# Making the low halves of two of four weight tiles with a negated copy on ScalarE and an adding DMA of GpSimd, in a two-block transformer kernel

## The chip, the cores and the metric

The kernel runs on one core of a Trainium2 chip. The metric is the device time of one execution in microseconds, the median of several runs. Beside it stands one profiled execution, whose span runs from the first to the last instruction.

## The reference

Two transformer blocks follow one another on one sequence of 512 tokens with 2048 channels, all in float32. What matters here is the first block and in it the "fox" attention: eight heads of width 128, each with four projections of the normalised input (query, key, value, output gate), causal scores with a bias from cumulated forget gates, a softmax, and the gated product.

```
h = rmsnorm(x, norm_g[l])
proj = h @ w_in[l]
cv_a, cv_b, cv_gate, fq, fk, fv, f_logit, fox_gate, mq, mem_gate = jnp.split(proj, SPLITS, axis=-1)
...
s = jnp.einsum('bqhd,bkhd->bhqk', qi, k) * scale
p = jax.nn.softmax(where(mask, s + bias, -inf), axis=-1)
y_fox = einsum('bhqk,bkhd->bqhd', p, v) * jax.nn.silu(fox_gate)
```

Beside it the first block has a causal convolution over 31 taps and an attention over a memory, and the second block a banded attention and a linear recurrence. Each column of every projection costs the same kind of work: a 2048 by 128 weight tile against all 512 tokens.

## The kernel before

**A product in three matmuls.** Float32 products are made from two rounded halves. A weight tile `raw` (128 partitions by 2048 floats, 1 MB) is split into `w_hi`, its rounding to the matmul's float32r, and `w_lo = raw - w_hi`. The input stands in SBUF as `act_hi` and `act_lo`. `project` on TensorE takes 16 steps over the channels with three matmuls each: `act_hi` by `w_hi`, `act_lo` by `w_hi`, `act_hi` by `w_lo`. It waits once, ahead of its first weight load, for the semaphore `w_split`, which counts whole split tiles. So a tile's low half must be there before its first matmul.

**How a tile comes in.** There are two slots of `raw`, `w_hi` and `w_lo`, used in turn. For tile t: SyncE loads `raw` (`load`, three tiles ahead, so it waits until tile t-2 is split, since that one stands in the same slot); ScalarE copies `raw` to `w_hi` (`split` in the scalar block) once TensorE has finished tile t-2; VectorE subtracts (`split` in the vector block) and counts `w_split` up; TensorE starts tile t when tile t-1 is through. Between the end of tile t-2 and the start of tile t lies one projection's time, or more where other matmuls are put between.

**A head of the fox phase.** It has four tiles, called 0 to 3 here; tile 4 is tile 0 of the next head. Each engine has its own program, a loop over the eight heads. `split(i, j)` makes tile j+1. Scores and transposes are put between the steps of tiles 2 and 3 (hooks), and `weigh`, the probabilities by the values, stands behind tile 3. VectorE has, beside the splits, the scaling of query and key, the softmax, four `ada_step` calls of two pieces (a product of a streamed weight of the second block with a vector, L2029), and convolution taps (L1868). SyncE's queue is in written order: `load` of tile 3 and its two `ada` pieces, `load` of tile 4 and two pieces, and so on. GpSimd has nothing in this phase.

Of the kernel before, what the change touches and what calls it, by code (L numbers as in the profile page):

```python
# [82 lines left out]
TILE0 = {}  # L83
# [69 lines left out]
def build(nc, wt, ada, bias, xT, memT, pw, cols_d, consts_d, starts_d, masks_d, spill, c_row, cum_rows, out):  # L153
    ctx = ExitStack()
    with ctx:
        def sb(name, shape, dt=F32, stack=ctx):
            return stack.enter_context(nc.sbuf_tensor(name, shape, dt))

        def sem(name):
            return ctx.enter_context(nc.semaphore(name))  # L160
# [10 lines left out]
        raw = sb("raw", [P, 2, D])  # L171
        w_hi = sb("w_hi", [P, 2, D], F32R)
        w_lo = sb("w_lo", [P, 2, D], F32R)
        cols = sb("cols", [P, NCOLS])
        consts = sb("consts", [P, CONSTS])
        masks = sb("masks", [P, 2 + NLEV, P], BF16)
# [123 lines left out]
        first_hi = sem("first_hi")  # L300
        first_split = sem("first_split")
        quad_done = sem("quad_done")
        s_x = [sem(f"s_x{n}") for n in range(4)]
        s_raw = [sem("s_raw0"), sem("s_raw1")]
        s_ada = [sem("s_ada0"), sem("s_ada1")]
        s_stage = [sem("s_stage0"), sem("s_stage1")]
# [134 lines left out]
                pair_turned)]  # L441
        own = {n: sem(f"own_{n}") for n in ("act", "dve", "pool")}

        s_block = [sem(f"s_block{n}") for n in range(4)]
        block_sum = Count(sem("block_sum"), fast=4)
        block_hi = Count(sem("block_hi"), fast=7)
        block_split = Count(sem("block_split"), fast=7)
# [52 lines left out]
        def tile_no(phase, i, j):  # L500
            return PHASES[phase][1] * i + (TILE0[phase] + j)
# [5 lines left out]
        def slot(phase, j):  # L507
            return (TILE0[phase] + j) % 2
# [689 lines left out]
        def _(act):  # L1198
# [4 lines left out]
            def split(phase, i, j, ahead=1):  # L1203
# [6 lines left out]
                act.wait_ge(proj_done, t if not isinstance(t, int) else max(t, 1))  # L1210
                fn(w_hi[:, s, :], raw[:, s, :], ACT.Copy).then_inc(w_hi_done, 1)  # L1211

            def rows(dst, src, width, tmp):

                o.step(fn(tmp, src, ACT.Ln, scale=1.0 / width, bias=eps_c))
                o.settle()
                return fn(dst, tmp, ACT.Exp, scale=-0.5)
# [183 lines left out]
            def fox(i):  # L1401
                split("fox", i, 0)
                split("fox", i, 1)
                high("fox", i, 0, qk_hi, qkv)
                split("fox", i, 2)
                high("fox", i, 1, qk_hi, qkv)
                for t in range(QT):
                    exps("fox", i, t, tp[:, 0, :])
                value_out("fox", i, 2, qkv[:, 2, :])
                split("fox", i, 3)  # L1410
                act.wait_ge(side_full.sem, side_full.at("fox", i, 1))
                o.step(fn(qkv[:, 3, S - P:S], ps_x[:, S - P:S], ACT.Copy))
                fn(v_hi[:, 0:S - P], ps_x[:, 0:S - P], ACT.Copy).then_inc(value_high.sem, 1)
                for j in range(QT):
                    probsT_fox(i, j)
                gate_exp("fox", i, 3, dst=2, src=wk[:, 1, :])
# [271 lines left out]
            def block_high(p, n):  # L1688

                if n in (1, 4, 6):  # L1690
                    f, k = ((0, 0), None, None, (0, 1), None, (1, 1))[n - 1]
                    if p:
                        act.wait_ge(s_block[2 * f + k], 16 * p)
                    else:
                        act.wait_ge(s_raw[slot("fast", f)], 16 * (half("fast", 0, f) + 1))
                else:
                    act.wait_ge(block_sum.sem, block_sum.at("fast", p, (2, None, 1, 3, None, 4)[n]))
                fast_slot_free(act, p, n)
                fn(fast_slot(n, w_hi), FAST_FROM[n], ACT.Copy).then_inc(block_hi.sem, 1)  # L1699
# [18 lines left out]
        def _(dve):  # L1718
# [325 lines left out]
                return TAPS_FOX * i + (TAPS0 + TAPS_MEM * NMEMH + n)  # L2044

            def fox(i):
                split("fox", i, 0)
                ada_step("fox", i, 0)
                conv_tap(fox_tap(i, 0))
                dve.wait_ge(proj_done, tile_no("fox", i, 0) + 2)  # L2050
                do(stt(qkv[:, 0, :], ps_p[:, slot("fox", 0), :], SCALE, r1[:, :], ALU.mult, ALU.mult))
                dve.sem_inc(evac[slot("fox", 0)], 1)
                dve.sem_inc(qk_in.sem, 1)
                split("fox", i, 1)
                ada_step("fox", i, 1)
                conv_tap(fox_tap(i, 1))
                low("fox", i, 0, qk_lo, qkv, qk_hi)
                o.settle()
                dve.wait_ge(proj_done, tile_no("fox", i, 1) + 2)
                do(tt(qkv[:, 1, :], ps_p[:, slot("fox", 1), :], r1[:, :], ALU.mult))  # L2060
                dve.sem_inc(evac[slot("fox", 1)], 1)
                dve.sem_inc(qk_in.sem, 1)
                dve.tensor_copy(tp[:, 1, 0:P], qkv[:, 1, 0:P]).then_inc(first_ready.sem, 1)
                split("fox", i, 2)
                dve.wait_ge(first_ready.sem, first_ready.at("fox", i, 1))
                low("fox", i, 1, qk_lo, qkv, qk_hi)
                o.settle()
                dve.sem_inc(qk_ready.sem, 1)
                for t in range(QT):
                    soft_in("fox", i, t, lambda t, e: stt(e, ps_s[:, t % 2, 0:P * (t + 1)], cn[:, t, bass.ds(i, 1)],  # L2070
                                                          Y[:, 4 + i, 0:P * (t + 1)], ALU.add, ALU.subtract))
                for t in range(QT):
                    soft_out("fox", i, t)
                ada_step("fox", i, 2)
                split("fox", i, 3)
                conv_tap(fox_tap(i, 2))
                value_lo("fox", i, v_lo, v_hi)
                for j in range(QT - 1):
                    dve.wait_ge(probsT_ready.sem, probsT_ready.at("fox", i, j + 1))
                    tt(p_lo[j], p_raw[j], turned(tp_r)[j].bitcast(F32), ALU.subtract).then_inc(probs_low.sem, 1)  # L2080
                silu_z("fox", i, 3, wk[:, 2, :], between=lambda: ada_step("fox", i, 3))
                ada_out("fox", i)
                dve.wait_ge(heads_full.sem, heads_full.at("fox", i, 1))
                tt(Y[:, 4 + i, :], ps_o[:, :], wk[:, 3, :], ALU.mult).then_inc(heads_done.sem, 1)
# [27 lines left out]

            dve.wait_ge(heads_done.sem, heads_done.at("fox", 7, 1))
            channels_added(Y)
            split("gate", 0, 0)
            dve.wait_ge(side_full.sem, side_full.at("gate", 0, 1))
            do(ts(ssq_b[:, :], ps_x[:, :], 1.0 / (NCONV * P), None, ALU.mult))
# [408 lines left out]
            def first_sums(p, n):  # L2526
                if n == 0:
                    if p:
                        dve.wait_ge(s_block[2], 16 * p)
                        dve.wait_ge(s_block[3], 16 * p)  # L2530
                        dve.wait_ge(block_split.sem, block_split.at("fast", p - 1, 5))
                    else:
                        for f in range(2):
                            dve.wait_ge(s_raw[slot("fast", f)], 16 * (half("fast", 0, f) + 1))
                    tt(block_sums[0], raw_block(1, 0), raw_block(1, 1), ALU.add).then_inc(block_sum.sem, 1)
                else:
                    if p:
                        dve.wait_ge(s_block[0], 16 * p)
                        dve.wait_ge(block_split.sem, block_split.at("fast", p - 1, 7))
                    dve.wait_ge(block_sum.sem, block_sum.at("fast", p, 1))  # L2540
                    tt(block_sums[1], block_sums[0], raw_block(0, 0), ALU.add).then_inc(block_sum.sem, 1)  # L2541

            def last_sums(p, n):
                if n == 2:
                    dve.wait_ge(block_split.sem, block_split.at("fast", p, 3))
                    tt(block_sums[0], raw_block(0, 0), raw_block(1, 0), ALU.add).then_inc(block_sum.sem, 1)
                else:
                    if p:
                        dve.wait_ge(s_block[1], 16 * p)
                    dve.wait_ge(block_split.sem, block_split.at("fast", p, 1))  # L2550
                    tt(block_sums[1], block_sums[1], raw_block(0, 1), ALU.add).then_inc(block_sum.sem, 1)

# [83 lines left out]
        def _(pool):  # L2636
# [19 lines left out]
            for k in range(KT):  # L2656
                if k % 4 == 0:
                    pool.wait_ge(s_mem[k // 4], 16)
                m = mem_raw[:, k, :]
                if k == 0:  # L2660
                    o.step(tt(mem_total, m, m, ALU.mult))
                    o.settle()
                    pool.sem_inc(mem_sq, 1)
                    pool.sem_inc(mem_added, 1)
                else:
                    o.step(tt(mem_norm, m, m, ALU.mult))
                    o.settle()
                    pool.sem_inc(mem_sq, 1)
                    o.step(tt(mem_total, mem_total, mem_norm, ALU.add))
                    o.settle()  # L2670
                    pool.sem_inc(mem_added, 1)

            def out1(i):

# [155 lines left out]
```

## Time and profile before

| | |
|---|---|
| median of 3 runs | 1859.9 us (1859.87 to 1860.23) |
| span of the profiled execution | 1857.9 us; 2.0 us lie around it |
| TensorE busy | 1851.6 us, 100% of the span |
| VectorE, ScalarE, GpSimd busy | 1285.2, 830.6, 210.6 us (69%, 45%, 11%) |
| fox phase | eight heads of 48.9 us, from about 251.9 to 643.4 us |
| HBM read | 235.75 MB |

Busy shares alone say which engine could be the bound, not which wait ends last at a given tile. That is read in the stretch of one head, from rows in order of time: a line there gives start, length, engine, source line, what is written from what, and in brackets the idle time before it and what ended it.

### The profile page before, as it was taken

What the parts mean: (1) busy time and instruction counts of PE and PEld (TensorE: products, weight loads), DVE (VectorE), ACT (ScalarE), POOL (GpSimd) and SP (SyncE); (2) the same over time, 40 slices, a digit from 0 to 9 for tenths busy, and PEclk for the clock granted to TensorE, in tenths of its full rate; (3) what the DMA queues carried; (4) which work ended last, traced back from release to release, by engine and by line L of the source; (5) the groups of instructions that cost most, each with busy time, mean ns of one, the idle gap of its engine ahead of it and who ended that gap; (6) DMA issues with size and microseconds to landing.
All of it is one profiled execution on the core that took longest, in us unless ns stands there. A gap on an engine that the chain in (4) does not pass through costs nothing.

```text
span 1857.9 us, 26478 instructions
## 1 busy us (share of the span) xinstructions
PE 1851.6 (100%) x9142; PEld 1553.5 (84%) x9142; DVE 1285.2 (69%) x1847; ACT 830.6 (45%) x1227; POOL 210.6 (11%) x203
## 2 busy tenths in 40 slices
PE   9999999999999999999999999999999999999999
PEld 8888888888888887887788888888888888888999
DVE  6766678888888877667844444455566666659986
ACT  6543433333333373233644444444555455557333
POOL 3500000000000003443000000000222222111111
PEclk9999999999999999999999999999999999999999
DMA  7344145444444435765222222221212212223442
GB/s 285 113 151 189 68 159 181 172 160 165 178 160 160 179 114 196 247 239 201 87 83 93 93 92 72 93 93 68 85 74 90 90 68 90 79 80 127 150 155 92
DMA packets 52002, 244.85 MB, mean 132 GB/s; under 512 B 5864, under 2 KB 7400, under 8 KB 32624
## 3 DMA queue, kind: packets, MB, share of 16 engines
q1 hardware_dynamic: 51504, 241.02, 36.7%
q10 hardware_dynamic: 448, 3.17, 0.4%
q8 instruction: 31, 0.51, 0.1%
q14 instruction: 19, 0.16, 0.0%
HBM read 235.75 MB, written 8.41 MB: 131 GB/s over the span
## 4 chain that ended last, share of the span: by engine, by line
PE 94%; DVE 4%; issue 1%; ACT 1%; POOLq 0%; DVEq 0%; another core or an unknown queue 0%; ACTq 0%
PE ps_p L729 25%; PE ps_p L731 25%; PE ps_p L730 25%; PE ps_o L894 1%; PE ps_s L1090 1%; PE ps_t L1188 1%; PE ps_t L1189 1%; PE ps_t L1187 1%; PE ps_t L878 1%; PE ps_s L1188 1%; PE ps_s L1187 1%; PE ps_s L1189 1%; PE ps_x L748 1%; DVE act_lo L2238 1%; PE ps_s L868 0%
## 5 line engine op out<-in xcount | busy, mean ns | idle before, releaser
L729 PE MATMUL ps_p<-act_hi,w_hi 128*128 128x512 f32 x2080 | 832.6, 400 | 0.3 <-DVE w_lo L1739 0.3
L731 PE MATMUL ps_p<-act_hi,w_lo 128*128 128x512 f32 x2080 | 812.0, 390 | 0.0
L730 PE MATMUL ps_p<-act_lo,w_hi 128*128 128x512 f32 x2080 | 810.6, 390 | 0.0
L731 PEld LDWEIGHTS ps_p<-act_hi,w_lo 128*128 128x128 f32 x2080 | 390.4, 188 | 85.2
L729 PEld LDWEIGHTS ps_p<-act_hi,w_hi 128*128 128x128 f32 x2080 | 391.0, 188 | 75.2 <-issue 1.2
L730 PEld LDWEIGHTS ps_p<-act_lo,w_hi 128*128 128x128 f32 x2080 | 391.4, 188 | 73.4 <-issue 0.7
L1211 ACT ACTIVATE w_hi<-raw 128x2048 fp32r<-128x2048 f32 x141 | 269.5, 1912 | 270.1 <-PE ps_p L731 251.4
L1734 DVE TENSOR_TENSOR w_lo<-raw,w_hi 128x2048 fp32r<-128x2048 f32 x139 | 318.7, 2293 | 72.2 <-ACT w_hi L1211 60.5
L2029 DVE CUSTOM_DVE_ANT_0 mkv<-mkv,c_all 128x1024 f32<-128x1024 f32 x96 | 146.0, 1557 | 3.3 <-DVE wk L1776 2.9
L2677 POOL TENSOR_TENSOR ssq_a<-ssq_a,wk 128x512 f32<-128x512 f32 x15 | 36.3, 2420 | 724.8 <-ACT wk L1475 724.8
L2697 POOL TENSOR_TENSOR hz<-hqk,hd 128x128 f32<-128x128 f32 x48 | 34.2, 713 | 728.6 <-DVEq L2403 690.0
L2251 DVE TENSOR_TENSOR sq_lo<-wk,sq_hi 128x512 fp32r<-128x512 f32 x24 | 16.6, 692 | 109.1 <-ACT sq_hi L1541 83.4
L1371 ACT ACTIVATE tp<-tp,stat 128x128 f32<-128x128 f32 (+1 forms) x64 | 35.9, 561 | 114.9 <-DVE stat L1998 114.9
L1868 DVE SCALAR_TENSOR_TENSOR Y<-upad,cols,Y 128x512 f32<-128x512 f32 x120 | 82.0, 745 | 0.0
L1744 DVE SCALAR_TENSOR_TENSOR wk<-ps_p,wk 128x512 f32<-128x512 f32 x23 | 15.9, 691 | 54.1 <-ACT wk L1228 54.1
L1699 ACT ACTIVATE w_hi<-mkv 128x1024 fp32r<-128x1024 f32 x24 | 25.5, 1061 | 62.1 <-DVE mkv L2541 32.9
L1539 ACT ACTIVATE wk<-ps_p 128x512 f32<-128x512 f32 x15 | 9.0, 597 | 85.1 <-PE ps_p L731 84.0
L1239 ACT ACTIVATE wk<-wk 128x512 f32<-128x512 f32 x43 | 27.2, 632 | 37.9 <-DVE wk L1783 20.5
L1626 ACT ACTIVATE hz<-hd 128x256 f32<-128x256 f32 x48 | 20.2, 422 | 49.5 <-DVE hd L2393 30.2
L1228 ACT ACTIVATE wk<-wk,cols 128x512 f32<-128x512 f32 (+1 forms) x53 | 38.4, 724 | 1.7
L1222 ACT ACTIVATE wk<-ps_p 128x512 f32<-128x512 f32 x32 | 19.0, 594 | 38.3 <-PE ps_p L731 38.3
L1226 ACT ACTIVATE wk<-wk 128x512 f32<-128x512 f32 (+1 forms) x53 | 33.5, 632 | 1.7
(435 smaller groups left out, 2578.5 us busy)
## 6 DMA issues: line engine op xcount, KB each, us to landing
raw<-wt_dram SPq DMA_DIRECT2D x146, 1024.0 KB, 4.8
mkv<-ada_dram SPq DMA_DIRECT2D x96, 512.0 KB, 4.4
raw<-wt_dram SPq DMA_DIRECT2D x20, 512.0 KB, 4.8
qkv<-xT_dram SPq DMA_DIRECT2D x16, 256.0 KB, 2.9
spill_dram<-Y SPq DMA_DIRECT2D x16, 256.0 KB, 2.2
out_dram<-wk SPq DMA_DIRECT2D x15, 256.0 KB, 2.1
Y<-xT_dram SPq DMA_DIRECT2D x3, 1024.0 KB, 10.7
mem_raw<-memT_dram SPq DMA_DIRECT2D x4, 512.0 KB, 11.9
```

The lines of the kernel that those rows point to most:

```text
L729: mm(o, wh, hi[:, k, 0:n], start=at == 0, stop=False)
L730: mm(o, wh, lo[:, k, 0:n], start=False, stop=False)
L731: last = mm(o, wl, hi[:, k, 0:n], start=False, stop=at == KT - 1)
L1187: mm(o, wh[:, c], hi[:, k, :], start=n < 3 and k == 0, stop=False, skip_group_check=True)
L1188: mm(o, wh[:, c], lo[:, k, :], start=False, stop=False, skip_group_check=True)
L1189: last = mm(o, wl[:, c], hi[:, k, :], start=False, stop=k == HALF_K - 1, skip_group_check=True)
L1211: fn(w_hi[:, s, :], raw[:, s, :], ACT.Copy).then_inc(w_hi_done, 1)
L1228: return fn(dst, dst, ACT.Ln, bias=one_c[0:dst.shape[0], :])
L1734: tt(w_lo[:, s, :], raw[:, s, :], w_hi[:, s, :].bitcast(F32), ALU.subtract).then_inc(w_split, 1)
L1868: o.step(stt(Y[:, c, :], upad[:, c, bass.ds(tap, S)], cols[:, bass.ds(tap + (w0 + c * TAPS), 1)], Y[:, c, :], ALU.mult, ALU.add))
L2029: dve.tensor_tensor_reduce(out=w, in0=w, in1=c_all[:, n % 2 * ADA_PIECE:(n % 2 + 1) * ADA_PIECE], scale=1.0, scalar=0.0, op0=ALU.mult, op1 ...
L2677: o.step(tt(ssq_a[:, :], ssq_a[:, :], wk[:, j, :], ALU.add))
```

## The change

For tiles 2 and 4 of each fox head VectorE no longer subtracts. ScalarE writes the negated rounding, `-w_hi`, into `w_lo` right behind its copy to `w_hi` (`negate`), and GpSimd issues a DMA from SBUF to SBUF that adds `raw` to `w_lo` (`accum_op=ALU.add`), waits for it to land, waits that the tile before has been counted, and counts `w_split` up. VectorE waits for that count before the splits that follow, so that the count stays in order. Tiles 1 and 3, and all other phases, are as before. To make room for two semaphores, the last phase takes over four that the memory's loads used (its waits are 16 higher), and an unused one is dropped.

```diff
+        ADDED = (1, 3)
-        s_block = [sem(f"s_block{n}") for n in range(4)]
+        s_block = s_mem
+        negated = Count(sem("negated"), fox=2)
+        s_low_added = sem("s_low_added")
...
+            def negate(phase, i, j):
+                s = (TILE0[phase] + j + 1) % 2
+                fn(w_lo[:, s, :], raw[:, s, :], ACT.Copy, scale=-1.0).then_inc(negated.sem, 1)
...
             def fox(i):
                 split("fox", i, 0)
                 split("fox", i, 1)
+                negate("fox", i, 1)
                 high("fox", i, 0, qk_hi, qkv)
...
                 split("fox", i, 3)
+                negate("fox", i, 3)
                 act.wait_ge(side_full.sem, side_full.at("fox", i, 1))
...
             def fox(i):
+                dve.wait_ge(w_split, tile_no("fox", i, 0) + 2)
                 split("fox", i, 0)
...
-                split("fox", i, 1)
                 ada_step("fox", i, 1)
...
+                dve.wait_ge(w_split, tile_no("fox", i, 2) + 2)
                 split("fox", i, 2)
...
                 ada_step("fox", i, 2)
-                split("fox", i, 3)
                 conv_tap(fox_tap(i, 2))
...
+            dve.wait_ge(w_split, tile_no("gate", 0, 0) + 2)
             split("gate", 0, 0)
...
+            def fox(i):
+
+                for n, j in enumerate(ADDED):
+                    s = slot("fox", j + 1)
+                    pool.wait_ge(negated.sem, negated.at("fox", i, n))
+                    pool.dma_start(w_lo[:, s, :], raw[:, s, :], accum_op=ALU.add).then_inc(s_low_added, 16)
+                    pool.wait_ge(s_low_added, 32 * i + 16 * n + 16)
+                    pool.wait_ge(w_split, tile_no("fox", i, j + 1) + 1)
+                    pool.sem_inc(w_split, 1)
+            for i in range(PHASES["fox"][0]):
+                fox(i)
```

**ScalarE, the first half of a fox head.** The rows below are the program of before, in order; `w_hi<-raw` is a split's copy, `qk_hi<-qkv` the rounding of the query, and `tp,stat` the first exponential.

```order
L1210 REGISTER_ALU [waits s_raw1]
L1211 ACTIVATE w_hi<-raw 128x2048 [waits proj_done]
L1397 REGISTER_ALU
L1399 ACTIVATE qk_hi<-qkv 128x384 [waits qk_in]
L1209 ISA
```

And the same place in the changed program.

```order
L1213 REGISTER_ALU [waits s_raw1]
L1214 ACTIVATE w_hi<-raw 128x2048 [waits proj_done]
L1218 ACTIVATE w_lo<-raw 128x2048
L1404 REGISTER_ALU
L1406 ACTIVATE qk_hi<-qkv 128x384 [waits qk_in]
```

A copy of the same shape, with no wait of its own, now stands between the split of tile 2 and the rounding of the query.

**ScalarE, the second half of a head.** The changed program around the split of tile 4; `v_hi` is the rounded value tile, `tp_r` the rounded transposed probabilities.

```order
L1214 ACTIVATE w_hi<-raw 128x2048 [waits own_act,proj_done,s_raw1]
L1218 ACTIVATE w_lo<-raw 128x2048
L1420 REGISTER_ALU
L1421 ACTIVATE qkv<-ps_x 128x128 [waits side_full]
L1422 ACTIVATE v_hi<-ps_x 128x384
```

The row of L1218 is new there too, ahead of `v_hi`.

**VectorE, around the key of a head.** Before, the split of tile 3 stands right behind the key's copy.

```order
L2060 TENSOR_TENSOR qkv<-ps_p,r 128x512 [waits proj_done,own_dve]
L2063 COPY tp<-qkv 128x128 [waits own_dve]
L1733 REGISTER_ALU
L1734 TENSOR_TENSOR w_lo<-raw,w_hi 128x2048 [waits w_hi_done]
```

Now it has a wait for tile 2's count ahead of it.

```order
L2069 TENSOR_TENSOR qkv<-ps_p,r 128x512 [waits proj_done,own_dve]
L2072 COPY tp<-qkv 128x128 [waits own_dve]
L2073 REGISTER_ALU
L1742 REGISTER_ALU [waits w_split]
L1743 TENSOR_TENSOR w_lo<-raw,w_hi 128x2048 [waits w_hi_done]
```

Two of a head's four rows of that shape on VectorE are gone (those of tiles 2 and 4), and both that stay wait for `w_split`.

## Rows read from the trace of the kernel before

**Rows 1.** Page: busy time and share; granted TensorE clock in 40 slices

```profile
PE 1851.6 (100%) x9142; PEld 1553.5 (84%) x9142; DVE 1285.2 (69%) x1847; ACT 830.6 (45%) x1227; POOL 210.6 (11%) x203
PEclk9999999999999999999999999999999999999999
```

**Rows 2.** Windows of a head each: engines' busy us, clock, DMA share, GB/s

```profile
545.50:594.50 49.00, 49.00 (x232) 40.75 (x230) 41.71 (x72) 18.43 (x29) 0.00 (x0) 1.00 0.49 171
...
sum 391.50, PE 391.50 PEld 325.44 DVE 330.99 ACT 146.76 POOL 0.00; mean PE 48.94 PEld 40.68 DVE 41.37 ACT 18.34 POOL 0.00
```

**Rows 3.** TensorE's waits, whole run: total us, times, longest (first and last)

```profile
PE ps_o L754 <- DVE wk L1720: 1.1, 1, 1.1
...
PE ps_o L1006 <- ACT wk L1501: 0.2, 1, 0.2
```

**Rows 4.** TensorE's weight loads that begin tile 2 and the next tile 0

```profile
567.18 0.19 PEld L729 LDWEIGHTS ps_p<-act_hi,w_hi 128*128 128x128 f32 x1
...
594.42 0.19 PEld L729 LDWEIGHTS ps_p<-act_hi,w_hi 128*128 128x128 f32 x1
```

**Rows 5.** ScalarE in order of time, one head

```profile
556.72 1.92 ACT L1211 ACTIVATE w_hi<-raw 128x2048 fp32r<-128x2048 f32 x1 [6.13 <-PE ps_p L731]
558.90 0.53 ACT L1399 ACTIVATE qk_hi<-qkv 128x384 fp32r<-128x384 f32 x1 [0.26 <-DVEq L2053]
...
582.65 1.92 ACT L1211 ACTIVATE w_hi<-raw 128x2048 fp32r<-128x2048 f32 x1 [0.25 <-ACT qkv L1387]
584.47 0.26 ACT L1412 ACTIVATE qkv<-ps_x 128x128 f32<-128x128 f32 x1
584.62 0.48 ACT L1413 ACTIVATE v_hi<-ps_x 128x384 fp32r<-128x384 f32 x1
586.74 0.69 ACT L1377 ACTIVATE tp_r<-ps_t,r1c 128x512 fp32r<-128x512 f32 x1 [1.63 <-PE ps_t L878]
...
588.36 0.59 ACT L1378 ACTIVATE tp<-ps_t,r1c 128x384 f32<-128x384 f32 x1
```

**Rows 6.** TensorE's transposes of probabilities, same head

```profile
589.89 0.27 PE L878 MATMUL ps_t<-consts,tp 128*128 128x128 f32 x1
```

**Rows 7.** VectorE in order of time, one head

```profile
559.03 2.29 DVE L1734 TENSOR_TENSOR w_lo<-raw,w_hi 128x2048 fp32r<-128x2048 f32 x1 [0.33 <-DVE qkv L2051]
...
566.19 0.55 DVE L1986 TENSOR_TENSOR qk_lo<-qkv,qk_hi 128x384 fp32r<-128x384 f32 x1
...
569.55 2.29 DVE L1734 TENSOR_TENSOR w_lo<-raw,w_hi 128x2048 fp32r<-128x2048 f32 x1 [0.71 <-ACT w_hi L1211]
```

**Rows 8.** VectorE's subtractions in the fox phase: duration ns min/median/max

```profile
L1734 DVE TENSOR_TENSOR w_lo<-raw,w_hi x32: 2281/2292/2294, 256.7 to 634.2; 128x2048 fp32r<-128x2048 f32 x32
```

**Rows 9.** Page: DMA issues, KB each, median us from issue to landing

```profile
raw<-wt_dram SPq DMA_DIRECT2D x146, 1024.0 KB, 4.8
mkv<-ada_dram SPq DMA_DIRECT2D x96, 512.0 KB, 4.4
```

**Rows 10.** SyncE's queue in order of time, one head

```profile
561.50 0.33 SPq L574 DMA_DIRECT2D raw<-wt_dram  x1
...
572.01 0.33 SPq L574 DMA_DIRECT2D raw<-wt_dram  x1
584.39 1.48 SPq L601 DMA_DIRECT2D mkv<-ada_dram  x2
587.74 0.33 SPq L574 DMA_DIRECT2D raw<-wt_dram  x1
```

**Rows 11.** Windows: one 1 MB load alone, then the stretch from 586.4

```profile
572.00:573.00 1.00, 1.00 (x8) 0.85 (x6) 0.45 (x1) 0.00 (x0) 0.00 (x0) 1.00 0.22 33
573.00:574.00 1.00, 1.00 (x9) 0.87 (x8) 0.56 (x2) 0.00 (x0) 0.00 (x0) 1.00 0.51 115
574.00:576.00 2.00, 2.00 (x12) 1.74 (x11) 1.77 (x7) 0.50 (x2) 0.00 (x0) 1.00 1.01 426
...
586.40:587.60 1.20, 1.20 (x10) 1.02 (x9) 1.20 (x2) 0.86 (x2) 0.00 (x0) 1.00 1.26 321
```

More of the change, by code:

```diff
@@ L302, in build @@
         quad_done = sem("quad_done")
-        s_x = [sem(f"s_x{n}") for n in range(4)]
+        s_x = [None, sem("s_x1"), sem("s_x2"), sem("s_x3")]
         s_raw = [sem("s_raw0"), sem("s_raw1")]
@@ L1692, in block_high @@
                     if p:
-                        act.wait_ge(s_block[2 * f + k], 16 * p)
+                        act.wait_ge(s_block[2 * f + k], 16 * p + 16)
                     else:
@@ L2528, in first_sums @@
                     if p:
-                        dve.wait_ge(s_block[2], 16 * p)
-                        dve.wait_ge(s_block[3], 16 * p)
+                        dve.wait_ge(s_block[2], 16 * p + 16)
+                        dve.wait_ge(s_block[3], 16 * p + 16)
                         dve.wait_ge(block_split.sem, block_split.at("fast", p - 1, 5))
@@ L2537, in first_sums @@
                     if p:
-                        dve.wait_ge(s_block[0], 16 * p)
+                        dve.wait_ge(s_block[0], 16 * p + 16)
                         dve.wait_ge(block_split.sem, block_split.at("fast", p - 1, 7))
@@ L2548, in last_sums @@
                     if p:
-                        dve.wait_ge(s_block[1], 16 * p)
+                        dve.wait_ge(s_block[1], 16 * p + 16)
                     dve.wait_ge(block_split.sem, block_split.at("fast", p, 1))
```

## The prediction, made before the changed kernel ran

> **What bounds the kernel now.** I read the busy shares first: TensorE is busy 1851.6 of 1857.9 us, and its granted clock stands in the top tenth in all 40 slices [rows 1]. VectorE, the engine that the change relieves, is at 69%. Busy shares are means over stages, so I then read the fox phase by itself. In each of the eight head windows TensorE is busy all the time, 391.50 of 391.50 us, VectorE 330.99, ScalarE 146.76, and GpSimd not at all [rows 2]. Last I read TensorE's waits. The whole run has six of them, from 1.1 us down to 0.2 [rows 3], and the same view over the fox phase alone has no line. So no low half comes late today. VectorE's subtraction for tile 2 runs from 559.03 to 561.32, and TensorE asks for that tile at 567.18, where it loads the first weights [rows 4, 7]. The slack is 5.9 us.
>
> From that follows the first half of the forecast: there is nothing to win at these sixteen tiles. A faster VectorE would end nothing sooner, because nobody waits for it. What the change can do is lose time, if the new way to the low half takes longer than its slack.
>
> **What is taken away.** Two subtractions a head of 2.292 us [rows 8], sixteen in all, 36.7 us of VectorE's time, none of it on the path. VectorE's work falls from 41.4 to about 36.8 us of a head's 48.9. I cost it at 0 both ways: the taps and pieces that follow only run earlier, and their ends are not waited for.
>
> **What ScalarE gets.** One more activation of the same shape as the copy, 1.92 us with the next one starting 1.82 us after it [rows 5], sixteen times. Cover: for tile 2 it runs from 558.54 to 560.46, so the rounding of the query moves from 558.90 to about 560.4. Its reader is the subtraction at 566.19 [rows 7], 5 us of room. For tile 4 it runs from 584.47 to 586.39. The value's two copies move from 584.47 to 586.3 and end near 586.95, where the first probabilities are taken at 586.74 now: 0.2 us later. Two copies further the end at 588.95 becomes 589.15, and the transpose that waits for it starts at 589.89 [rows 5, 6]. So 0.7 us of room is left; I cost it at 0. If it were gone, each tenth of a microsecond of lateness would be 0.8 us over eight heads.
>
> **What the DMA has to meet.** Tile 2: the negated copy ends at 560.46 and TensorE asks at 567.18, so 6.7 us remain for GpSimd to wake, issue, move 1 MB with an addition, see it land and count. Tile 4: 586.39 to 594.42, 8.0 us [rows 4, 5]. This is the term on which all rests, and no trace row shows it: there is no DMA of GpSimd, none from SBUF to SBUF and none that adds. I bound it by the nearest row, SyncE's load of the same 1 MB: 4.8 us from issue to landing [rows 9]. The load at 572.01 [rows 10] shows what these 4.8 us are made of. For about 1 us hardly anything moves, for another 1 us the DMA engines are half busy at 115 GB/s, and then they stream at 426 GB/s, at which 1 MB is 2.46 us [rows 11].
>
> Lower bound: it costs what a load costs, 4.8 us, landing at 565.3, 1.9 us ahead of need. Upper bound by rows: an addition has to read both its operands, so the stream is twice as long, 4.8 + 2.46 = 7.3 us; with some 0.1 us for GpSimd's counting, tile 2 comes 0.7 us late. At tile 4 two `ada` pieces are issued just ahead, by 585.9, and the engines are full with them until 587.6 and beyond [rows 10, 11]. I put 1 us on it: 586.39 + 8.3 + 0.1 = 594.8, 0.4 us late. That is 1.1 us a head, 8.8 us in all.
>
> Between them I take the doubled stream without most of the slow second microsecond, since the source is not HBM, about 0.6 us less, but with GpSimd's issue 0.2 us dearer than SyncE's: 6.9 us. Tile 2 is ready at 567.4 to 567.5, 0.2 to 0.3 us late; tile 4 at 594.4, on time. Eight heads at 0.25 us are 2 us at most, and half of that if the first weight load hides behind the matmuls still in flight. I take +1.2 us.
>
> The Trainium skill bears on this twice. Its page "Collectives: The Full Stack" (Part 3, on the bandwidth ceiling) says that the reduce step runs at half the rate of the copy step because the adding descriptor has two source reads on the same ring, not because the addition costs anything. No run here shows it yet; by it the stream is the doubled one. Its page "DMA: Bandwidth & Descriptors" (Anatomy of one DMA) gives for GpSimd's DMAs 2.0 us plus bytes by 436 GB/s, which with two reads of 1 MB is an estimate of 6.8 us, and it (SWDGE vs HWDGE) speaks against the change in that only GpSimd's software path can accumulate at all, with a first byte at about 1 us against 0.6.
>
> **What waits behind the new waits.** VectorE's split of tile 3 now waits for tile 2's count. It starts at 569.55 today [rows 7], so a DMA that lands by 569.5 does not hold it; behind it stand the key's low half and the softmax, which the scores between tile 2's steps need. On SyncE, the load of tile 4 goes from 561.50 to about 567.4 and that of the tile after next from 587.74 to about 594.4 [rows 10], and the `ada` pieces behind them with it. The first is read at 582.65, 15 us later; the second by the next head's split at 605.66, one head of 48.94 us behind the row at 556.72 [rows 2, 5], 11 us later. With 4.8 us to land both are hidden. The later load also leaves the DMA engines to the adding transfer. The `ada` pieces behind the second come up to one load's stream, 2.46 us, later than now; VectorE, which reads them, has 4.6 us a head to spare. I cost it at 0.
>
> **The sum.** Span 1857.9 + 0 (VectorE) + 0 (ScalarE) + 1.2 (DMA) = 1859.1 us, and with the 2.0 us that lie between span and median, 1861.1 us. What a measurement of this kernel can tell from no change is about 0.2%, 3.7 us.
>
> **Rivals.**
> *Late by the whole doubled stream or somewhat more.* If neither the start-up nor anything else is saved, 8.8 us come on top as worked out, 1868.7 us; with 1 us more for GpSimd's issue, 2 us more per head, 1885. For it: the doubled stream is plain, and the slack of tile 2 is only 6.7 us. It decides slower from 0.47 us of lateness per head on, a DMA of about 7.1 us. This is the rival on the other side. Chance 0.34.
> *The adding DMA is another kind of slow* (its engines do not stream at 426 GB/s at all). If its stream took four times a copy's, 9.8 us, the DMA is 12.2 us: tile 2 late by 5.6, tile 4 by 5.3, some 11 us a head, 87 us in all, 1947. Nothing in the trace speaks for it, nothing excludes it. At three times, 1908. Chance 0.12.
> *VectorE's relief shows somewhere.* It would need TensorE to be held by VectorE in the fox phase or at its end. TensorE has no wait in this phase, and the longest of the run is 1.1 us [rows 3]. If that one went, it would be 1859.9 - 1.1 = 1858.8 us. Chance of more than 0.2%: 0.03.
> *ScalarE's added copy holds the scores or transposes.* The room is 0.7 us, and at 1 us of extra lateness it would cost 2.4 us; it lies within the first two cases.
>
> **How the numbers follow.** Just in time or all but, within 0.2%: 0.51, and its own range is 1859.4 to 1863.6. Late by up to 2 to 3 us a head: 0.34, 1863.6 to 1885. Much later: 0.12. Faster by over 0.2%: 0.03. The range of 8 in 10 runs from 1859.3 to 1885: below it is hardly anything, above it the third case and the tail of the second. Faster 0.03, same 0.51, slower 0.46.
>
> **What would show it.** In the fox windows of the changed kernel VectorE's busy time falls to about 36.8 us a head and ScalarE's rises to about 22.3. GpSimd's DMAs appear, 16 of 1 MB, with about 6.9 us to landing: 4.8 would say one read is enough, 7.3 the upper bound, over 9 the third case. TensorE's waits have a line for the first matmul of a tile, released by GpSimd, of some tenths of a microsecond and at most 16 times, or none. If waits of over 0.5 us stand there, the rival holds; if the wait falls on a score or a transpose instead, the ScalarE step is wrong. A granted clock below the top tenth in these slices would be something that I have left out.

## The result and the profile after

The changed kernel takes 1872.3 us (median of 4 runs, 1871.33 to 1872.81) against 1860.07 us (1859.87 to 1860.68): the ratio is 1.0066, 95% interval 1.0051 to 1.008, some 12.2 us slower. The profiled execution has a span of 1869.5 us, 11.6 us more than before, at a granted clock of 1.0.

The page of the changed kernel, to be read against [rows 1, 9]: busy time, the queue of GpSimd's DMAs (packets, MB, share of 16 engines), and issues with median us to landing.

```profile
PE 1856.3 (99%) x9142; PEld 1554.1 (83%) x9142; DVE 1251.7 (67%) x1831; ACT 857.5 (46%) x1243; POOL 224.7 (12%) x219
...
q0 software_dynamic: 2304, 16.78, 4.4%
...
raw<-wt_dram SPq DMA_DIRECT2D x146, 1024.0 KB, 4.8
mkv<-ada_dram SPq DMA_DIRECT2D x96, 512.0 KB, 5.4
w_lo<-raw POOLq DMA_DIRECT2D x16, 1024.0 KB, 7.6
```

VectorE is busy 33.5 us less, where 36.7 us of subtractions were taken away; no run looked into the other 3 us. TensorE became busier by 4.7 us with the same 9142 matmuls, and its span grew by 11.6. A matmul that starts behind a pause shows a longer time, so busy time alone does not show where the rest went. TensorE's waits over the fox phase, an empty answer before, do:

```profile
PE ps_p L732 <- POOLq L2691: 7.3, 16, 0.9
```

L732 is the first matmul of a projection step and L2691 GpSimd's count of `w_split`. The row gives total, number of waits and the longest, and all sixteen tiles are waited for. One head in order of time, tile 2 first, from ScalarE's and GpSimd's rows and TensorE's matmuls and weight loads:

```profile
567.48 1.90 ACT L1218 ACTIVATE w_lo<-raw 128x2048 fp32r<-128x2048 f32 x1
...
569.67 0.86 POOL L2688 DMA_DIRECT2D w_lo<-raw  x1 [22.96 <-ACT w_lo L1218]
...
576.11 0.39 PE L734 MATMUL ps_p<-act_hi,w_lo 128*128 128x512 f32 x1
576.68 0.50 PE L732 MATMUL ps_p<-act_hi,w_hi 128*128 128x512 f32 x1 [0.19 <-POOLq L2691]
...
576.68 0.19 PEld L732 LDWEIGHTS ps_p<-act_hi,w_hi 128*128 128x128 f32 x1 [0.61 <-POOLq L2691]
```

The negated copy ends at 569.38 and GpSimd's DMA starts at 569.67: 0.29 us go for the wake-up. The next matmul follows after 0.57 us instead of the usual 0.23, so 0.34 us are lost ahead of it, and another 0.11 us behind it, where the matmul after it starts 0.34 us later instead of 0.23. The bracket on the matmul says only 0.19, because the one before it is still drawn as running. The weight load's bracket says 0.61. Before, that load started together with the last matmul of the tile ahead [rows 4]; now it starts with its own matmul. So a wait row gives less than the loss: 7.3 us in the list. The starts of the matmuls themselves give 4.05 us at tile 2's eight places and 7.53 at tile 4's, together the 11.6 us of the span.

Then tile 4 of the same head:

```profile
596.08 0.86 POOL L2688 DMA_DIRECT2D w_lo<-raw  x1 [25.55 <-ACT w_lo L1218]
...
603.72 0.38 PE L900 MATMUL ps_o<-tp,qkv 128*128 128x128 f32 x2
604.44 0.49 PE L732 MATMUL ps_p<-act_hi,w_hi 128*128 128x512 f32 x1 [0.34 <-POOLq L2691]
```

0.72 us between these two starts, where it was 0.14; this is the mildest of the eight. How long the DMAs take tells the two tiles apart: 6.9 to 7.0 us at tile 2, 8.2 to 8.8 at tile 4. The line of GpSimd's issue gives shortest, median and longest of all sixteen, and the windows show the DMA engines, first for tile 2's DMA and then for tile 4's. A window's line gives its stretch and length, the busy time of TensorE's matmuls and weight loads, VectorE, ScalarE and GpSimd, the clock, the DMA engines' share and the GB/s.

```profile
DMA to landing us min/median/max: 6.9/7.6/8.8
...
569.70:571.10 1.40, 1.40 (x7) 1.15 (x7) 1.40 (x3) 0.08 (x1) 0.83 (x1) 1.00 0.03 6
571.10:576.30 5.20, 5.20 (x24) 4.13 (x22) 2.74 (x5) 0.00 (x0) 0.00 (x0) 1.00 0.99 200
...
596.10:598.00 1.90, 1.90 (x12) 1.54 (x11) 1.80 (x4) 1.90 (x5) 0.84 (x1) 1.00 0.93 257
598.00:604.00 6.00, 6.00 (x32) 4.98 (x30) 2.88 (x5) 2.44 (x6) 0.00 (x0) 1.00 0.91 203
```

At tile 2 next to nothing moves for 1.4 us after the issue. Then the engines are full for 5.2 us, and the view credits them with 200 GB/s, where a load ran at 426 [rows 11]. 1 MB at 200 GB/s is 5.2 us, twice a load's 2.46. At tile 4 the engines are at work already when the DMA is issued.

### The profile page after: what moved, and what is told of

Read it like the earlier page. It is cut to its first block, busy times and chain, and to the rows that moved or that the text cites. A ratio compares the mean times of both kernels' runs of the same rounds, so it can differ in the third digit from the quotient of the medians.

```text
span 1869.5 us, 26503 instructions
## 1 busy us (share of the span) xinstructions
PE 1856.3 (99%) x9142; PEld 1554.1 (83%) x9142; DVE 1251.7 (67%) x1831; ACT 857.5 (46%) x1243; POOL 224.7 (12%) x219
## 3 DMA queue, kind: packets, MB, share of 16 engines
q0 software_dynamic: 2304, 16.78, 4.4%
## 4 chain that ended last, share of the span: by engine, by line
PE 60%; DVE 4%; ACT 1%; issue 1%; DVEq 0%; another core or an unknown queue 0%; ACTq 0%
PE ps_p L732 16%; PE ps_p L734 16%; PE ps_p L733 16%; PE ps_s L1093 1%; PE ps_t L1191 1%; PE ps_t L1192 1%; PE ps_t L1190 1%; PE ps_s L1191 1%; PE ps_s L1190 1%; PE ps_s L1192 1%; PE ps_o L897 1%; DVE act_lo L2248 1%; PE ps_t L881 0%; DVE w_lo L2565 0%; ACT act_hi L1654 0%
## 5 line engine op out<-in xcount | busy, mean ns | idle before, releaser
L732 PE MATMUL ps_p<-act_hi,w_hi 128*128 128x512 f32 x2080 | 833.6, 401 | 7.7 <-POOLq L2691 7.3
L732 PEld LDWEIGHTS ps_p<-act_hi,w_hi 128*128 128x128 f32 x2080 | 391.0, 188 | 87.2 <-issue 7.1
L1743 DVE TENSOR_TENSOR w_lo<-raw,w_hi 128x2048 fp32r<-128x2048 f32 x123 | 282.1, 2293 | 70.0 <-ACT w_hi L1214 59.9
L2038 DVE CUSTOM_DVE_ANT_0 mkv<-mkv,c_all 128x1024 f32<-128x1024 f32 x96 | 146.6, 1557 | 15.2 <-DMA mkv<-ada_dram 11.8
L2688 POOL DMA_DIRECT2D w_lo<-raw x16 | 13.9, 868 | 554.4 <-ACT w_lo L1218 554.4
```

The source lines that it names most:

```text
L732: mm(o, wh, hi[:, k, 0:n], start=at == 0, stop=False)
L1743: tt(w_lo[:, s, :], raw[:, s, :], w_hi[:, s, :].bitcast(F32), ALU.subtract).then_inc(w_split, 1)
L2038: dve.tensor_tensor_reduce(out=w, in0=w, in1=c_all[:, n % 2 * ADA_PIECE:(n % 2 + 1) * ADA_PIECE], scale=1.0, scalar=0.0, op0=ALU.mult, op1 ...
```

## The experiments

Theory A: the loss is the adding DMA's lateness at TensorE, tile by tile. Theory B: ScalarE's added copies do it. The third question was whether VectorE's freed time is worth anything. Every kernel was timed beside the kernel before on the same chip; its median there was 1860.03 to 1860.10 us.

### One tile at a time

```diff
-        ADDED = (1, 3)
+        ADDED = (1,)
...
-                negate("fox", i, 3)
...
                 ada_step("fox", i, 2)
+                split("fox", i, 3)
```

> Only tile 2 of each head gets its low half by the adding DMA; VectorE subtracts tile 4 again. Theory A, the loss is the lateness of the DMA, tile by tile: in the changed kernel's trace the eight gaps ahead of tile 2 are 0.34 to 0.52 us longer than a normal step, and the matmul after each comes 0.11 us later, together about 4.0 us, so 1860.1 + 4.0 = 1864.1 us. GpSimd's DMA takes 6.9 us as before. Theory B, ScalarE's added copies hold the scores or transposes and the waits only look like the DMA's: half of the loss, 1866, and the gaps ahead of tile 2 change. If the two tiles' losses were not additive, this and the run with tile 4 alone would not sum to 12.2 us.

Measured: 1864.37 us, ratio 1.0023 (1.0014 to 1.0032), 4.3 us lost. The eight DMAs take 6.9 to 7.0 us, and the waits row is

```profile
PE ps_p L732 <- POOLq L2691: 1.9, 8, 0.4
```

The reverse, `ADDED = (3,)` with VectorE's `split("fox", i, 1)` put back:

> Only tile 4 of each head gets its low half by the adding DMA; VectorE subtracts tile 2 again. Theory A: the gaps ahead of tile 4 in the changed kernel were 0.6 to 1.2 us against 0.14 normally, in sum 6.5 us and some 0.9 more behind them, so about 1867.6 us; the DMA takes 8.2 to 8.8 us there, because two ada pieces are in the DMA engines with it. Theory B: 1866.

Measured: 1866.31 us, ratio 1.0032 (1.002 to 1.0044), 6.3 us lost, DMAs of 7.9 to 8.8 us. The first is near theory A's 1864.1 and not theory B's 1866. The second lies 1.3 us under theory A's 1867.6 and next to theory B's 1866, so by its size it does not tell the two apart. That is done by two runs further below, the plain copy and ScalarE's copies alone. The two losses sum to 10.6 us, not 12.2. The 1.6 us between are less than the intervals of these runs, some 2 us each way, and in the profiled executions nothing is left over: their spans are 4.5 and 7.7 us longer than before, and 11.6 with both.

### A copy instead of an addition

```diff
-                    pool.dma_start(w_lo[:, s, :], raw[:, s, :], accum_op=ALU.add).then_inc(s_low_added, 16)
+                    pool.dma_start(w_lo[:, s, :], raw[:, s, :]).then_inc(s_low_added, 16)
```

> The DMA of GpSimd copies raw into w_lo and does not add, so the low halves of these sixteen tiles are wrong and the output is not the reference's; everything else stays. Theory A with the doubled read: the packets go from 0.64 us to about 0.31, the DMA from 6.9 to about 4.4 us at tile 2 and from 8.4 to about 6 at tile 4, no wait of TensorE is left, 1860.1 us. Rival, the cost is GpSimd's software issue or the conversion to float32r and not the second read: packets stay at 0.6 us and the time at 1872.

Measured: 1859.99 us, ratio 0.9999 (0.999 to 1.0008). The loss is gone. The DMA's share in the page, the issue's line, and the windows of one DMA at tile 2:

```profile
q0 software_dynamic: 2304, 16.78, 2.3%
...
L2688 POOL DMA_DIRECT2D w_lo<-raw x16: 530/530/722, 267.2 to 635.6; - x16
...
DMA to landing us min/median/max: 4.1/5.1/6.5
...
560.70:561.80 1.10, 1.10 (x7) 0.90 (x6) 1.09 (x3) 0.14 (x1) 0.53 (x1) 1.00 0.00 0
561.80:564.50 2.70, 2.70 (x14) 2.23 (x13) 2.70 (x6) 0.00 (x0) 0.00 (x0) 1.00 1.00 388
```

Same source, same target, same conversion to float32r, same issuer, same 2304 packets: the addition alone raises the stream from 2.7 to 5.2 us and the start from 1.1 to 1.4. The issue itself takes 530 ns against 859. So an adding DMA of 1 MB costs 2.8 us more than a copying one (6.9 against 4.1). The run does not tell whether it is the second read or the adding itself that doubles the stream.

### The negated copy first

```diff
                 act.wait_ge(proj_done, t if not isinstance(t, int) else max(t, 1))
+                if negated_first:
+                    negate(phase, i, j)
                 fn(w_hi[:, s, :], raw[:, s, :], ACT.Copy).then_inc(w_hi_done, 1)
...
-                split("fox", i, 1)
-                negate("fox", i, 1)
+                split("fox", i, 1, negated_first=True)
...
                     pool.wait_ge(w_split, tile_no("fox", i, j + 1) + 1)
+                    pool.wait_ge(w_hi_done, tile_no("fox", i, j + 1) + 2)
                     pool.sem_inc(w_split, 1)
```

(`split("fox", i, 3)` likewise.)

> Both tiles by the adding DMA as in the changed kernel, but ScalarE writes the negated copy first and w_hi behind it, so the DMA starts 1.8 us earlier and w_hi is ready 1.8 us later, still 4.8 us ahead of need. Theory A: tile 2 is then 1.3 us early and tile 4 about 0.9 us early, no wait is left, and the time is that of the kernel before, 1860.1 us; VectorE's 36.7 us less work win nothing. Rival, VectorE's relief is worth something that the waits hid: clearly under 1860. Theory B, ScalarE's extra copy costs by itself: it stays at 1866 or more, as ScalarE has the same work at the same places.

Measured: 1860.69 us, ratio 1.0004 (0.9995 to 1.0013). All sixteen adding DMAs are there, the list of TensorE's waits in the fox phase is empty, and the time is that of the kernel before within the interval. The page:

```profile
PE 1852.8 (100%) x9142; PEld 1554.1 (84%) x9142; DVE 1251.5 (67%) x1831; ACT 857.7 (46%) x1243; POOL 224.5 (12%) x219
...
w_lo<-raw POOLq DMA_DIRECT2D x16, 1024.0 KB, 8.8
```

The DMAs are even slower here than in the changed kernel, 8.8 us in the median against 7.6. They start while more of the other loads are under way: at tile 4 of the head shown above the two `ada` pieces are issued 0.5 us ahead of the DMA instead of 2.3. They cost next to nothing all the same, because they start 1.8 us earlier. The list leaves out short waits; by the matmuls' starts three of the eight tiles 4 still come late. The first and worst, 0.43 us between two starts instead of 0.14:

```profile
300.90 0.38 PE L900 MATMUL ps_o<-tp,qkv 128*128 128x128 f32 x2
301.33 0.49 PE L732 MATMUL ps_p<-act_hi,w_hi 128*128 128x512 f32 x1
```

The three add up to 0.6 us. So even the swapped order has no room left at tile 4. And VectorE is relieved by the same 34 us as in the changed kernel, with no gain.

### The `ada` pieces out of the way

```diff
-                    ada_piece(ADA_PER[phase] * i + (ADA_G0[phase] + n + 2), n % 2)
+                    ada_piece(ADA_PER[phase] * i + (ADA_G0[phase] + n + 2), n % 2, 128 if phase == "fox" and j == 2 else ADA_PIECE)
```

> The changed kernel, with the two ada pieces that SyncE loads just ahead of tile 4's adding DMA cut from 1024 to 128 columns each, so the second block's modulation is computed from stale numbers and the output is not the reference's. Theory A with contention: tile 4's DMA takes 6.9 to 7.1 us, as tile 2's does, instead of 8.2 to 8.8, lands ahead of need, and only tile 2's waits are left: 1864.1 us. Rival, tile 4's DMA is longer for another reason (ScalarE's and VectorE's work beside it): it stays at 8.4 us and 1872.

Measured: 1864.43 us, ratio 1.0023 (1.0013 to 1.0032), and the issue's line and the waits row are

```profile
DMA to landing us min/median/max: 6.9/6.9/7.0
...
PE ps_p L732 <- POOLq L2691: 1.8, 8, 0.4
```

All sixteen DMAs now take the 6.9 us of one alone, tile 4 is in time, and tile 2's loss stays, 4.3 us, as in the run with tile 2 alone. ScalarE's and VectorE's work beside tile 4's DMA is that of the changed kernel, so it is not what makes that DMA longer.

### In halves

```diff
-                fn(w_lo[:, s, :], raw[:, s, :], ACT.Copy, scale=-1.0).then_inc(negated.sem, 1)
+                for c in (slice(0, BLOCK), slice(BLOCK, D)):
+                    fn(w_lo[:, s, c], raw[:, s, c], ACT.Copy, scale=-1.0).then_inc(negated.sem, 1)
...
+                    for h, c in enumerate((slice(0, BLOCK), slice(BLOCK, D))):
+                        pool.wait_ge(negated.sem, negated.at("fox", i, 2 * n + h))
+                        pool.dma_start(w_lo[:, s, c], raw[:, s, c], accum_op=ALU.add).then_inc((s_low_added, s_low_second)[h], 16)
                     pool.wait_ge(s_low_added, 32 * i + 16 * n + 16)
+                    pool.wait_ge(s_low_second, 32 * i + 16 * n + 16)
```

> The negated copy in two halves of 1024 columns and an adding DMA of 512 KB behind each, so the first starts some 0.9 us earlier. If the stream of packets is what takes the time: both halves together land about 0.7 us earlier, tile 2 is in time and tile 4 late by 0.3, 1860.1 + 2.5 = 1862.6 us. Rival, each DMA of GpSimd pays its start of 1.4 us in turn and ScalarE pays for two shorter copies: no gain, 1872 or more.

Measured: 1871.57 us, ratio 1.006 (1.0046 to 1.0074). A miss: the total is near the rival's 1872, but its cause does not fit either, since tile 2 does gain. The waits row and two rows of GpSimd and TensorE:

```profile
PE ps_p L733 <- POOLq L2695: 10.8, 8, 1.6
...
595.89 1.81 POOL L2691 DMA_DIRECT2D w_lo<-raw  x2 [24.12 <-ACT w_lo L1220]
...
605.99 0.49 PE L733 MATMUL ps_p<-act_hi,w_hi 128*128 128x512 f32 x1 [1.21 <-POOLq L2695]
```

Only tile 4 is still waited for: at tile 2 the earlier start works. At tile 4 ScalarE's split began at 592.73 here and at 592.06 in the changed kernel. Counted from it the first DMA is issued after 3.16 us instead of 4.02, yet TensorE starts after 13.26 instead of 12.38. A start 0.9 us earlier ended 0.9 us later. The windows from the first issue on show where the time goes:

```profile
595.90:597.00 1.10, 1.10 (x8) 0.92 (x8) 1.10 (x3) 1.10 (x4) 1.01 (x2) 1.00 0.91 361
597.00:598.00 1.00, 1.00 (x8) 0.82 (x7) 1.00 (x2) 1.00 (x3) 0.70 (x1) 1.00 1.44 139
598.00:599.00 1.00, 1.00 (x6) 0.78 (x5) 0.75 (x3) 1.00 (x3) 0.00 (x0) 1.00 0.37 94
```

From 597 to 599 little moves, 139 and 94 GB/s. The adding DMA's first packet comes at 598.99, 3.1 us after its issue; at tile 2 of this kernel it comes after 1.4 us, and at tile 4 of the changed kernel after 1.5 to 2.2. So at tile 4 the halves lose their lead in a late start of the stream. What holds the stream back beside the `ada` pieces stays open.

### ScalarE's copies alone

```diff
                 split("fox", i, 1)
+                negate("fox", i, 1)
...
+                dve.wait_ge(negated.sem, negated.at("fox", i, 0))
                 split("fox", i, 1)
```

(the same at tile 4, on the kernel before)

> The kernel before, with ScalarE's sixteen negated copies into w_lo added at the places of the changed kernel; VectorE waits for each and then subtracts over it, there is no DMA of GpSimd. The two splits of VectorE come up to 1.5 us later. Theory A: nothing waits for either, 1860.1 us. Theory B, the added copies delay the query's rounding, the value and the transposes: up to 1866, with waits of TensorE on scores, transposes or values.

Measured: 1860.71 us, ratio 1.0004 (0.9994 to 1.0013). TensorE is busy through the whole phase, with ScalarE at 173.22 us against 146.76 [rows 2]:

```profile
251.90:643.40 391.50, 391.50 (x1826) 325.46 (x1825) 330.57 (x562) 173.22 (x242) 0.00 (x0) 1.00 0.47 169
```

So theory B is out: the copies by themselves cost nothing that this run can tell from noise.

### The tile with the most room

Tile 3 alone, `ADDED = (2,)`, with `negate("fox", i, 2)` behind the key's rounding and the three other subtractions on VectorE.

> Only tile 3 of each head gets its low half by the adding DMA; VectorE subtracts the others. Tile 3 has the longest room, since scores stand between the steps of tile 2: the negated copy ends about 573.3 in the time frame of the kernel before, the DMA takes 6.9 us, no ada piece is in its way, and TensorE asks at about 581.5. Theory A, only the room counts: it lands by 580.6, no wait, 1860.1 us. Rival, at this place ScalarE's copy does hold the key's rounding and with it the second scores: waits of TensorE on a score, and 1861.5 or more.

Measured: 1860.9 us, ratio 1.0005 (0.9996 to 1.0014), DMAs of 6.9 to 7.7 us, no wait in the fox phase. At this tile the DMA fits as it is.

### Tile 2 in time, tile 4 as it was

The negated copy goes first for tile 2 alone; tile 4 is as in the changed kernel.

> Both tiles by the adding DMA; ScalarE negates first for tile 2 alone, so that tile 2's DMA is there but in time, and tile 4 is as in the changed kernel. Tile 4 alone cost 6.3 us, both together 12.2, tile 2 alone 4.3, so 1.6 us are left over. If they come from tile 2 being late (it shifts what follows in the head), this run loses 6.3 us, 1866.3. If they come from tile 2's DMA being there at all (it holds SyncE's loads back, so that ada pieces come later), it loses about 7.9 us, 1868.0.

Measured: 1866.17 us, ratio 1.0033 (1.002 to 1.0045). 6.1 us lost, as with tile 4 alone. The median is next to the first expectation, 1866.3, but the interval, 3.7 to 8.4 us lost, holds the second too, so the run does not decide what the 1.6 us are, or whether they are more than scatter. Tile 4's DMA takes 8.5 us in the mean of eight in the changed kernel, 8.4 here and 8.3 with tile 4 alone, and from head to head it varies by more than that (8.2 to 8.8, 8.2 to 8.6 and 7.9 to 8.8 us).

## Why the prediction was right in part

**The bound and the missing gain were right.** TensorE was full in this phase and nobody waited for the sixteen subtractions. Two kernels that keep VectorE's relief and have no late DMA, or three by 0.1 to 0.3 us, take 1860.69 (negated first) and 1859.99 us (plain copy), like the kernel before. So the rival that VectorE's relief shows somewhere is refuted, and the 33.4 to 33.7 us that VectorE is busy less in them are worth nothing here.

**ScalarE's copy at 0 was right**, shown by its run alone.

**The DMA was sized right and judged late by too little.** I had taken 6.9 us between 4.8 and 7.3, and alone it takes 6.9 to 7.0. Its doubled stream is shown by the plain copy, and what the Trainium skill says in "Collectives: The Full Stack" on the two source reads fits with that trace, 5.2 us against 2.7; no run separates the second read from the adding. What failed is the step from there to "Tile 2 is ready at 567.4 to 567.5, 0.2 to 0.3 us late; tile 4 at 594.4, on time", and the 1.2 us put on it. Three terms were too small or missing:

- The wake-up of GpSimd, 0.29 us from the end of the copy to the issue. I had only 0.1 us, for the count at the end.
- Tile 2: with it the loss is 4.3 us over eight heads, 0.54 a head against 0.25 at most. With the wake-up put in, the prediction's own slack gives it: in the head shown the weight load comes 0.57 us later than it could (576.68 instead of 576.11). The assumption that half would hide behind the matmuls in flight was wrong, since 0.45 us of these 0.57 are lost: 0.34 ahead of the first matmul and 0.11 behind it.
- Tile 4: two `ada` pieces ahead of it cost 1.0 to 1.9 us (7.9 to 8.8 against 6.9), not 1.0. This was the larger error: 6.3 us with tile 4 alone where the sum had 0. That the pieces do it is shown by the run with small pieces, where tile 4 is in time.

**The outcome was the first rival**, "late by the whole doubled stream or somewhat more", given 0.34, with 8.8 us and up; 12.2 were measured. It lies in the range. That the range held is partly luck: its upper part was made for a start-up that is not saved and a dearer issue, and what filled it was the wake-up and the `ada` pieces. The likeliest case fell because its edge was 0.47 us of lateness a head, no more than the terms that were too small, and all of these had the same sign.

**What waits behind the new waits was right in cost and wrong in a detail.** TensorE waits for nothing but GpSimd's count in this phase, so SyncE's later loads of `raw` cost nothing. VectorE did wait for `ada` pieces, 11.8 us against 0.2 in the whole run, inside its new room: with the negated copy first it waits 15.1 us for them, and the time is that of the kernel before.

## What to carry to other kernels

Before work is moved from an engine that nobody waits for, ask what the new way's latency is against the old one's slack: here there was nothing to win and 6.7 us to keep within. A chain through a copy, another engine's wake-up, a DMA and a count has to be summed with every hand-over, at the longest case, with what else is in the DMA engines at that moment. If it just misses, first look for an order that starts it earlier: one swap of two ScalarE copies gave back 11.6 of the 12.2 us, while cutting the DMA in two did not.

## What the runs showed of the hardware that was not expected

- An adding DMA from SBUF to SBUF of 1 MB took 6.9 us from issue to landing, a copying one of the same shape from 4.1: stream 5.2 against 2.7 us, start 1.4 against 1.1, issue instruction 0.86 against 0.53.
- The time lost at a wait is more than its row says: 16 waits, 7.3 us listed, 11.6 us more span. And a wait can be missing from the list: three late starts of 0.1 to 0.3 us in the negated-first kernel have no row.
- An adding DMA that shared the engines with 1 MB of loads took up to 9.6 us (the negated-first kernel). Split in two halves, of which the first started 0.9 us earlier, it ended 0.9 us later beside them: its first packet came 3.1 us after the issue, where it came after 1.4 with the engines free.
